# Delta-rule output formed with tokens on the partitions, and VectorE's queue reordered, in a chunked decoder kernel

## The reference, cut to what matters

```python
v_new = u_n - jnp.einsum('bhck,bhkv->bhcv', w_n, s)
o_n = jnp.einsum('bhck,bhkv->bhcv', qd_n, s) + jnp.einsum('bhij,bhjv->bhiv', a_n, v_new)
s = s * gl_n[..., None, None] + jnp.einsum('bhck,bhcv->bhkv', kd_n, v_new)
...
o = o * lax.rsqrt(jnp.mean(o * o, axis=-1, keepdims=True) + NORM_EPS) * p['gdn_norm_w'].astype(f32)
o_a = (o * jax.nn.silu(za.astype(f32).reshape(b, L, H_A, HD_A))).reshape(b, L, D_A)
```

## Time and profile before

| | |
|---|---|
| time, median of 3 runs | 1240.06 us (1239.82 to 1240.42) |
| the profiled execution's own time | 1239.08 us |
| its span in the trace | 1237.4 us |
| granted TensorE clock, mean over the span | 0.98 |
| TensorE busy (matmul) | 94% of the span |
| prompt stage, chunks 0 to 7 | about 457 to 648 us |

### The profile page before, as it was taken

How to read it: one execution, slowest core, us unless ns; L and a number is a source line. 1 busy time by engine, 2 the same in 40 slices (tenths; PEclk the granted TensorE clock), 3 DMA queues, 4 the chain that set the end, 5 groups by cost and what they waited for, 6 DMA issues and landing times. The chain is left out here.

```text
span 1237.4 us, 31587 instructions
## 1 busy us (share of the span) xinstructions
PE 1169.1 (94%) x12762; PEld 840.0 (68%) x12762; DVE 519.7 (42%) x1250; ACT 336.8 (27%) x785; POOL 565.0 (46%) x821
## 2 busy tenths in 40 slices
PE   9999999999999999999999999679999999999990
PEld 7788878756666677787754545357777777777760
DVE  3456987655394525645523113532222222222223
ACT  5002112342441245564423222201111111111114
POOL 7412221110840248788632021046666666666661
PEclk9999999999999999999999999889999999999995
DMA  7301120124103110000075214499999897997838
GB/s 213 102 1 36 36 69 18 35 88 145 34 19 94 52 20 17 23 16 18 21 238 181 86 69 136 133 345 372 307 373 329 269 374 231 297 375 255 273 51 297
DMA packets 142875, 187.14 MB, mean 151 GB/s; under 512 B 39464, under 2 KB 89247, under 8 KB 142778
## 3 DMA queue, kind: packets, MB, share of 16 engines
q1 hardware_dynamic: 126010, 164.87, 39.1%
q0 software_dynamic: 15936, 20.57, 8.1%
q10 hardware_dynamic: 832, 0.33, 0.1%
HBM read 156.41 MB, written 29.32 MB: 150 GB/s over the span
## 5 line engine op out<-in xcount | busy, mean ns | idle before, releaser
L527 PE MATMUL ps<-hT,w_in 128*128 128x352 f32 (+1 forms) x624 | 189.3, 462 | 1.8 <-ACT cb L807 1.2
L527 PEld LDWEIGHTS ps<-hT,w_in 128*128 128x128 f32 x624 | 117.5, 190 | 69.0 <-issue 4.0
L3125 POOL DMA_INDIRECT sum_rows<-slot_out,scatter_rows x76 | 122.0, 1605 | 38.7 <-POOL scatter_rows L3124 26.0
L3257 DVE TENSOR_TENSOR slot_T<-slot_raw_T,vecs 128x256 f32<-128x256 f32 x75 | 32.5, 433 | 211.8 <-PE ps L3170 211.8
L3170 PE MATMUL ps<-qkv,slot_T 128*32 128x256 f32 x1920 | 111.6, 383 | 4.5 <-DVE slot_T L3257 3.7
L3170 PEld LDWEIGHTS ps<-qkv,slot_T 128*32 128x32 f32 x1920 | 75.6, 111 | 34.3 <-DVE slot_T L3257 5.2
L3102 POOL DMA_INDIRECT gathered<-h_rows,gather_rows x79 | 83.7, 1060 | 19.1 <-issue 12.2
L3214 ACT ACTIVATE slot_silu<-ps 128x128 f32<-128x128 f32 x77 | 21.5, 279 | 226.7 <-PE ps L3170 224.4
L3170 PE MATMUL ps<-cb,slot_T 128*32 128x256 f32 x1408 | 80.6, 379 | 0.0
L3170 PEld LDWEIGHTS ps<-cb,slot_T 128*32 128x32 f32 x1408 | 55.4, 110 | 20.5
L3220 ACT ACTIVATE slot_out<-ps,slot_weights 128x256 f32<-128x256 f32 x76 | 36.1, 475 | 111.9 <-PE ps L3181 111.9
(11 more groups left out here) (764 smaller groups left out, 2383.5 us busy)
## 6 DMA issues: line engine op xcount, KB each, us to landing
qkv<-in_expert_w_gate SPq DMA_DIRECT2D x6, 2048.0 KB
qkv<-in_expert_w_up SPq DMA_DIRECT2D x6, 2048.0 KB
qkv<-in_expert_w_down SPq DMA_DIRECT2D x6, 2048.0 KB
cb<-in_expert_w_gate SPq DMA_DIRECT2D x5, 2048.0 KB
cb<-in_expert_w_up SPq DMA_DIRECT2D x5, 2048.0 KB
zg<-in_expert_w_down SPq DMA_DIRECT2D x5, 2048.0 KB
third_w_down<-in_expert_w_down SPq DMA_DIRECT2D x5, 2048.0 KB
w_in<-in_w_in SPq DMA_DIRECT2D x18, 512.0 KB, 4.7
```

The lines of the kernel that those rows point to most:

```text
L527: last = pe.matmul(pbank(b)[:, c, 0:n], w[:, k, :], hT[:, k, c * CH:c * CH + n], start=(k == 0), stop=(k == KD - 1))
L3125: pool.indirect_dma_start(quarter_sums, bass.IndirectOffsetOnAxis(ap=sidx[:, r:r + 1], axis=0), y[r][:], None, compute_op=ALU.add).then_in ...
L3257: dve.tensor_tensor(xT[:], xr[:], bc(nf, 2, ROWS_SLOT), ALU.mult).then_inc(s.xT, 1)
```

## The change

The product order of `o` is swapped, so that bank 6 holds tokens on the partitions and channels along the free axis. ACT still squares it; VectorE sums the squares along the free axis to 128x4 (`squares_sum`); ACT forms the inverse roots of these 4 columns, now ahead of `exps` in its queue; VectorE multiplies bank 6 by them into `sq` (`normed`); TensorE turns `sq` back with four transposes into bank 7 (`turned`); VectorE's `gated` reads bank 7 and finishes `g.zg`, so GpSimd's product goes. In VectorE's queue `state_A` and `gated` move to the end of the body. `norm_sum` goes; `kd @ S` no longer waits for `rs`; the Grams wait for `gated` of the chunk before, `keys` waits for `normed`.

```diff
@@ -1353,7 +1353,7 @@
 
 
 PROMPT_SEMS = """init gq0 gq1 scan aex e123 el rkb krk dtp dexp kqd gram lta0 ltA atT tokT tokc gramK evK gramB lb0 lb1 near0 near1 nz nT
-YA YC mA mC UA UC uA uC tfA tfC trv vtok trk kdec ks X xq xc pp pc vn vnew dz y1 yc z zp dS o sqo og Sup osum rs ymu yd sqy yvar yrs bon xb bv odA odC
+YA YC mA mC UA UC uA uC tfA tfC trv vtok trk kdec ks X xq xc pp pc vn vnew dz y1 yc z zp dS o sqo on oT Sup osum rs ymu yd sqy yvar yrs bon xb bv odA odC
 stT fin""".split()
 
 
@@ -1371,6 +1371,7 @@
     Z, Zp = sb("Z", P, 2, P), sb("Z_decayed", P, 2, P)
     dm, ndm, ea, el = (sb(k, P, 2, NT) for k in ("mid", "minus_mid", "end", "chunk_decay"))
     LTA, LTC = sb("LTA", P, H, P), sb("LTC", P, H, P)
+    os, oln = sb("o_scale", P, H), sb("o_log", P, H)
     def in_hT(name, k, col, *shape):
         return place("p_" + name, 4032 + k * NEXT + col, *shape)
 
@@ -1497,9 +1498,6 @@
                 if t >= 0:
                     differences(e)
             if t >= 0:
-                pool.wait_ge(s.og, t + 1)
-                pool.wait_ge(s.rs, t + 1)
-                pool.tensor_tensor(g.zg[:, :, cols(t)], g.zg[:, :, cols(t)], sq[:], ALU.mult).then_inc(s.odA, 1)
                 pool.wait_ge(s.yrs, t + 1)
                 pool.tensor_tensor(yd[:], yd[:], sy[:], ALU.mult)
                 pool.drain()
@@ -1534,7 +1532,6 @@
                     pe.wait_ge(pr.zte, 3)
                 if t >= 1:
                     pe.wait_ge(s.Sup, t)
-                    pe.wait_ge(s.rs, t)
                 for h in range(H):
                     last = pe.matmul(bank(4)[:, h, :], kd[:, h, :], S[:, h, :], start=True, stop=True)
                 last.then_inc(s.ks, 1)
@@ -1553,6 +1550,8 @@
                 if u >= 1:
                     pe.wait_ge(s.kdec, u)
                     pe.wait_ge(s.vtok, u)
+                if u >= 2:
+                    pe.wait_ge(s.odA, u - 1)
                 for h in range(H):
                     pe.matmul(bank(6)[:, h, :], g.qkv[:, 4 + h, c], g.qkv[:, 4 + h, c], start=True, stop=True)
                     last = pe.matmul(bank(7)[:, h, :], g.qkv[:, 4 + h, c], g.qkv[:, h, c], start=True, stop=True)
@@ -1632,14 +1631,16 @@
                 if prep:
                     pe.wait_ge(s.lta0, nxt)
                 for h in range(H):
-                    pe.matmul(bank(6)[:, h, :], vnew[:, h, :], at[t % 2][:, h, :], start=True, stop=False)
-                    last = pe.matmul(bank(6)[:, h, :], S[:, h, :], gq[t % 2][:, h, :], start=False, stop=True)
+                    pe.matmul(bank(6)[:, h, :], at[t % 2][:, h, :], vnew[:, h, :], start=True, stop=False)
+                    last = pe.matmul(bank(6)[:, h, :], gq[t % 2][:, h, :], S[:, h, :], start=False, stop=True)
                 last.then_inc(s.o, 1)
 
-            def norm_sum():
-                pe.wait_ge(s.sqo, now)
-                pe.wait_ge(s.Sup, now)
-                pe.matmul(ps[:, 4, :], m.ones[:], flat(sq[:]), start=True, stop=True).then_inc(s.osum, 1)
+            def turned():
+                pe.wait_ge(s.on, now)
+                pe.wait_ge(s.vtok, min(nxt, NT))
+                for h in range(H):
+                    last = pe.transpose(bank(7)[:, h, :], sq[:, h, :], m.ident[:])
+                last.then_inc(s.oT, 1)
 
             def y_mean():
                 pe.wait_ge(s.yc, now)
@@ -1661,8 +1662,8 @@
                 pe.wait_ge(s.odA, 1)
                 pe.wait_ge(s.odC, 1)
                 first_rows(0, 0, 4)
-                norm_sum()
                 y_mean()
+                turned()
                 first_rows(0, 4, 6)
                 bonus()
                 first_rows(0, 6, KD)
@@ -1678,7 +1679,7 @@
             def keys():
                 if state:
                     pe.wait_ge(s.sqo, now)
-                    pe.wait_ge(s.og, now)
+                    pe.wait_ge(s.on, now)
                 else:
                     pe.wait_ge(s.lta0, nxt)
                 for h in range(H):
@@ -1832,6 +1833,11 @@
                 if state:
                     act.wait_ge(s.X, now)
                 act.activation(vtok[:], bank(7), ACT.Copy).then_inc(s.vtok, 1)
+            if state:
+                act.wait_ge(s.osum, now)
+                act.activation(oln[:], os[:], ACT.Ln, scale=1.0 / HA, bias=NORM_EPS)
+                act.drain()
+                act.activation(os[:], oln[:], ACT.Exp, scale=-0.5).then_inc(s.rs, 1)
             if e < NT and state:
                 exps(act, e)
             if state:
@@ -1848,10 +1854,6 @@
                 exps(act, e)
                 act.wait_ge(s.init, 1)
             if state:
-                act.wait_ge(s.osum, now)
-                act.activation(flat(sq[:]), ps[:, 4, :], ACT.Ln, scale=1.0 / HA, bias=NORM_EPS)
-                act.drain()
-                act.activation(sq[:], sq[:], ACT.Exp, scale=-0.5).then_inc(s.rs, 1)
                 act.wait_ge(s.yvar, now)
                 act.activation(flat(sy[:]), ps[:, 5, 0:256], ACT.Ln, scale=1.0 / HC, bias=GN_EPS)
                 act.drain()
@@ -1952,9 +1954,17 @@
                 transposed(TC, TTs["C"][u % 2]).then_inc(s.nT, 1)
                 transposed(TA, TTs["A"][u % 2]).then_inc(s.nT, 1)
 
+            def squares_sum():
+                dve.wait_ge(s.sqo, now)
+                dve.tensor_reduce(os[:], sq[:], AX_X, ALU.add).then_inc(s.osum, 1)
+
+            def normed():
+                dve.wait_ge(s.rs, now)
+                dve.tensor_tensor(sq[:], bank(6), bc(os[:], 2, P), ALU.mult).then_inc(s.on, 1)
+
             def gated():
-                dve.wait_ge(s.sqo, now)
-                dve.scalar_tensor_tensor(g.zg[:, :, cols(t)], bank(6), g.vec("gdn_norm_w"), g.zg[:, :, cols(t)], ALU.mult, ALU.mult).then_inc(s.og, 1)
+                dve.wait_ge(s.oT, now)
+                dve.scalar_tensor_tensor(g.zg[:, :, cols(t)], bank(7), g.vec("gdn_norm_w"), g.zg[:, :, cols(t)], ALU.mult, ALU.mult).then_inc(s.odA, 1)
 
             def state_A():
                 dve.wait_ge(s.dS, now)
@@ -1973,19 +1983,22 @@
                 dve.tensor_tensor(rk[:], two(ps[:, 5, 256:512]), g.cb[:, 4:6, cols(t)], ALU.mult).then_inc(s.bv, 1)
 
             if not prep:
+                squares_sum()
+                state_A()
+                normed()
+                centred()
                 gated()
-                state_A()
-                centred()
                 bonus_v()
                 continue
             TTA, TTC = TTs["A"][u % 2], TTs["C"][u % 2]
+            if state:
+                squares_sum()
             dve.wait_ge(s.YC, 2 * u + 1)
             copy_join(yx[1], 2).then_inc(s.mC, 1)
             dve.wait_ge(s.YA, 2 * u + 1)
             copy_join(yx[0], 0).then_inc(s.mA, 1)
             if state:
-                gated()
-                state_A()
+                normed()
             dve.wait_ge(s.UC, 2 * u + 1)
             join_low(TC, 2).then_inc(s.uC, 1)
             join_T(TTC, 2)
@@ -2000,6 +2013,8 @@
             top_copy(TA, 1).then_inc(s.mA, 1)
             if state:
                 bonus_v()
+                state_A()
+                gated()
         dve.wait_ge(s.stT, 1)
         dve.tensor_copy(flat(Zp[:]), ps[:, 2, 0:256]).then_inc(s.fin, 1)
 
```

## The result

The changed kernel takes 1243.58 us (median of 14 runs, 1240.97 to 1246.93) where the kernel before, run beside it, took 1241.01 (14 runs, 1239.82 to 1241.91). The ratio is 1.0024, 95% interval 1.0017 to 1.0031: slower, by about 3.0 us by the ratio and 2.6 between the medians. The profiled execution took 1240.97 us, 1.9 more than before's, with a span of 1239.2, 1.8 more. It is the shortest of the 14.

What follows compares the result with a forecast made beforehand. TensorE's stream was taken as the bound, its chunks held after the change by `exps` and GpSimd's chain to decay_exps. 6 × 0.59 − 1.06 − 0.4 = +2.1 us gave 1242.1, range 1241.2 to 1243.2, 8-in-10 range 1239.3 to 1246.0.

Steps and rivals of the forecast that it cites:

- The bound: Prompt stage: ACT's order releases decay_exps before the change, GpSimd's chain after; that chain had 0.18 us of slack.
- `exps` at 1.74, decay_exps at 9.59, the first product with the inverse at 13.29, chunk 23.95: Six prompt chunks, us after ACT's square: `exps` start 0.77 later, each chunk takes +0.59, together +3.5.
- `kd @ S` at 7.1: TensorE in a chunk: starts about 7.1 us after the square, not 8.48; this 1.4 lost again before line 1566.
- The last interval: Chunk 6, which prepares no `exps`: line 1566 comes at 10.6 instead of 11.66, −1.06 us.
- The last chunk: Chunk 7: TensorE swaps about 1.0 us of sum of squares for 0.44 to 0.66 of transposes, −0.4.
- GpSimd and VectorE's queue: Prompt stage: GpSimd losing its 512-column product costs and gains nothing; the Grams' new wait for `gated` costs nothing.
- The sum: Whole kernel: 6 × 0.59 − 1.06 − 0.4 = +2.1 us, 1242.1 against the median, +0.17%.
- Rival A: VectorE's scan blocks GpSimd's differences in six chunks: +1.6 to +4.6 us, 1243.7 to 1246.7; chance 0.22.
- Rival B: Small activations on ACT or semaphores are dearer: +0.2 us a chunk, 1243.4; chance 0.07.
- Rivals C and D: C: `exps` not late, 1237.5, chance 0.08; D: chunk follows TensorE and ACT alone, decay_exps at 7.96, 1232.3, chance 0.04.

Runs made afterwards that it cites:

- experiments 2 and 3: GpSimd's differences moved ahead of its keys: in the changed kernel (2) 1234.2 us, ratio 0.9946; in the kernel before (3) ratio 1.0002.
- Experiment 4: Changed kernel with a second pair of small Ln and Exp on ACT between the roots and `exps`: 1248.4 us, ratio 1.0082.
- experiment 6: Changed kernel with `state_A` back in the middle of VectorE's queue, directly behind `normed`: 1243.65 us, ratio 1.0030.
- experiment 8: Changed kernel with differences ahead of keys on GpSimd and decay_exps ahead of mixer C's roots on ACT: 1233.5 us, ratio 0.9943.
- experiment 5: Changed kernel with six unread identity products on TensorE ahead of line 1565, filling its idle time: median 1243.0 us, ratio 1.0023.
- experiment 10: Kernel before with differences ahead of keys on GpSimd and decay_exps ahead of mixer C's root on ACT: ratio 1.0030.

## Why the prediction was right, point by point

- **The bound.** Right. decay_exps were released by the GpSimd chain in the changed kernel and by ACT's own order before; experiments 2 and 3 separate the two. One thing the prediction passed over: before, TensorE's own stream ended at the same point. Its last Gram products there ended as line 1566 began, at 531.88 and without idle time, so an earlier XC alone would have won next to nothing. The row of before's trace:

```profile
531.53 0.39 PE L1558 MATMUL ps<-qkv 128*128 128x128 f32 x2
```

- **`exps` at 1.74, decay_exps at 9.59, the first product with the inverse at 13.29, chunk 23.95.** Measured 1.74, 9.58, 13.29, 23.95. The reduction took 0.69 (0.68 taken), the small pair 0.39. Experiment 4 shows the slope: 0.54 more ahead of `exps` gave chunks 0.6 longer, 0.56 where no scan ran beside the differences.
- **`kd @ S` at 7.1** and its 1.3 lost again: 7.18, with 1.68 of idle time in front of line 1565 (up to 2 taken). From the transposes to the next product it was 0.53 where 0.44 was taken.
- **The last interval,** −1.06: −0.96, line 1565 at 10.71 for 10.6. The root of mixer C started at 7.28 for 7.20.
- **The last chunk,** −0.4: −0.41. w_out landed in time; first_rows followed `o` without a wait.
- **GpSimd and VectorE's queue:** nothing, as said; experiment 6 shows that the reordering pays only in the last interval.
- **The sum,** +2.1 and 1242.1: the traces give +2.16, the ratio about +3.0 (2.1 to 3.8). The median of before was itself 1241.01 over more runs and not 1240.06, which is 0.95 of the 1.48 between 1242.1 and 1243.58. So 1243.58 lies 0.4 above the forecast's own range, 1241.2 to 1243.2, and inside only the wider one, 1239.3 to 1246.0, which had been drawn for rivals that did not come about. The change came out just above 0.2%, where 0.48 had been given to "within" and 0.44 to "slower": the mechanism was right, the side of that bound was not foretold.
- **Rival A** (scan blocks the differences) did not come about: in the changed kernel scan started 0.14 behind the start of the last of the differences, which together took 2.81 for 2.79, and itself took 0.84 for 0.76. Where scan did start amid them, in experiment 4, they lost 0.10, not 0.27. The Trainium skill's exclusion (SBUF — State Buffer, Who interferes with whom) would have made scan wait in experiment 4 for the third of the differences to end, another 0.45 us; it started during it and the pair took 0.73. For the differences, then, the measurement differs from the Trainium skill. It agrees better beside a GpSimd product of two SBUF tiles: in experiment 8 the first scan instruction began with 0.59 us of such a product left to run, and took 0.86 where it takes 0.42 in before's trace.

```profile
526.99 0.73 POOL L1500 TENSOR_TENSOR p_y_centred<-p_y_centred,p_y_squares 128x256 f32<-128x256 f32 x1
527.13 0.86 DVE L1881 TENSOR_TENSOR_SCAN p_acum<-ones,lw 128x128 f32<-128x128 f32 x1
```

- **Rival B:** the small activations took 0.21 and the pair 0.39. The 0.3 us each that the Trainium skill (ScalarE: Activation LUTs, Rules for kernel authors) budgets is given there for a bias passed as a `[128,1]` operand. The code of these two passes constants, so the prediction's estimate of 0.6 by that row did not apply to them.
- **Rivals C and D** were refuted by the chunk's 23.95; D's shape, and more than its gain, came with the two moves of experiment 8.
- **What the prediction lacked** is the clock. It priced idle time of TensorE at its own length. In four experiments single chunks or intervals lost another 0.4 to 3.6 us to stretches at 1.2 GHz. No such stretch is in the prompt stage of any of the four traces of the changed kernel, so it is not shown that it makes the 0.8 us between +2.16 and +3.0, and that part stays open. For the longest single times the runs speak against it: 6 us lost at half clock would lower the mean granted clock by about 0.005 (an estimate, 12 us at 0.5 in 1240), and the two longest executions, 1246.93 and 1246.81, have the same 0.977 as the shortest, 1240.97. The filling in experiment 5 did not remove the spread either, and its trace shows that the start of the stage and the stages behind it vary by as much as one fall costs.

## What to carry to other kernels

When two chains end within 0.2 us of each other, lengthening the one to shorten the other is free only up to that slack. Look for what stands first in an in-order queue: here a wait and 0.39 us of small roots, placed ahead of `exps`, cost 0.59 a chunk, while taking 1.22 us of large roots off the same queue further back won nothing as long as GpSimd's chain held decay_exps. The time lost in the stage came back, and 7.1 us more, by letting GpSimd do first what needs no input from ACT. When reordering to use freed time, list every reader of a buffer that is written next: the missed wait in experiment 10 cost 0.62 a chunk, as much as the change.

## What the hardware showed that was not expected

Short waits of TensorE were followed by a stretch at half clock, in some executions and some chunks only. Behind 2.33 us of idle time two of six chunks had 3.3 us at 0.5 (+1.65 each), behind 0.94 one interval (+1.63), during or behind 1.5 to 1.6 next to the 32-row joins five of six had 7 to 10 us (+2.3 to +3.6); behind 1.68 none in 24 chunks traced. What decides it is not settled by these runs.

The small activations over 128x4 take 0.21 us and follow each other, with a drain, in 0.27. What a VectorE scan and a GpSimd instruction cost each other differed by the GpSimd instruction: 0.08 (on scan) and 0.10 (on GpSimd) beside the differences, 0.27 on line 1507's first instruction, 0.44 on scan beside a product of two SBUF tiles that had 0.59 left to run.
